# Prompt attention of a hybrid decoder step: each score matmul issued two steps ahead of its transpose instead of one, with three score buffers, and the first scores moved to an earlier place

## What is computed

```python
def masked_softmax(s, mask):
    s = jnp.where(mask, s, NEG)
    m = jnp.max(s, axis=-1, keepdims=True)
    p = jnp.where(mask, jnp.exp(s - m), 0.0)
    return p / jnp.maximum(jnp.sum(p, axis=-1, keepdims=True), 1e-30)
...
    s = jnp.einsum('bqgrd,bkgd->bqgrk', q_b, kv_b[:, :, 0], preferred_element_type=f32) * ATTN_SCALE
    s = s - slopes[None, None, :, :, None] * dist[None, :, None, None, :]
    p = masked_softmax(s, mask)
    o = jnp.einsum('bqgrk,bkgd->bqgrd', p, kv_b[:, :, 1].astype(f32))
...
    o = g[:, :, 0] * o_cmp + g[:, :, 1] * o_sel + g[:, :, 2] * o_win
```

## Time and profile before

| | us |
|---|---|
| median of 3 runs (2410.17 to 2414.91) | 2412.21 |
| the profiled execution | 2410.67 |
| its span, first to last instruction | 2409.0 |
| PE busy in the span | 2229.3 |
| the prompt attention, first to last of its jobs | 1310.0 to 1683.9 |

### The profile page before, as it was taken

How to read it: one execution, slowest core, us unless ns; L and a number is a source line. 1 busy time by engine, 2 the same in 40 slices (tenths; PEclk the granted TensorE clock), 3 DMA queues, 4 the chain that set the end, 5 groups by cost and what they waited for, 6 DMA issues and landing times. The chain is left out here.

```text
span 2409.0 us, 53122 instructions
## 1 busy us (share of the span) xinstructions
PE 2229.3 (93%) x22026; PEld 2038.8 (85%) x22026; DVE 1260.8 (52%) x2504; ACT 823.1 (34%) x1519; POOL 279.3 (12%) x430
## 2 busy tenths in 40 slices
PE   7999999999999999999998888788889769999997
PEld 6998888888888888999997666677887559999997
DVE  6345555555555553588883456565145425355454
ACT  4333334333333422222223344344223224233342
POOL 0000000000000100001004233111314410000000
PEclk9999999999999999999998899899999879999999
DMA  4322121221212222786756222211749954445564
GB/s 146 104 73 78 51 65 56 65 78 55 73 52 64 75 77 75 254 289 219 253 191 194 66 70 65 72 56 42 272 156 322 301 170 147 134 137 172 185 202 140
DMA packets 139540, 318.98 MB, mean 132 GB/s; under 512 B 28090, under 2 KB 56996, under 8 KB 138276
## 3 DMA queue, kind: packets, MB, share of 16 engines
q1 hardware_dynamic: 102148, 226.72, 29.3%
q0 software_dynamic: 17040, 55.63, 7.0%
q10 hardware_dynamic: 20112, 33.23, 4.0%
HBM read 277.77 MB, written 46.06 MB: 134 GB/s over the span
## 5 line engine op out<-in xcount | busy, mean ns | idle before, releaser
L200 PE MATMUL acc<-xh,w_hi 128*128 128x272 f32 x2944 | 657.6, 305 | 11.4 <-DVE w_lo L168 10.4
L200 PE MATMUL acc<-xh,w_lo 128*128 128x272 f32 x2944 | 616.3, 291 | 0.0
L200 PE MATMUL acc<-xl,w_hi 128*128 128x272 f32 x2944 | 616.2, 291 | 0.0
L200 PEld LDWEIGHTS acc<-xh,w_hi 128*128 128x128 f32 x2944 | 465.9, 192 | 67.2 <-issue 45.7
L200 PEld LDWEIGHTS acc<-xl,w_hi 128*128 128x128 f32 x2944 | 471.0, 192 | 0.0
L200 PEld LDWEIGHTS acc<-xh,w_lo 128*128 128x128 f32 x2944 | 468.6, 192 | 0.0
L168 DVE TENSOR_TENSOR w_lo<-w_raw,w_hi 128x1024 fp32r<-128x1024 f32 x164 | 200.2, 1223 | 206.8 <-ACT w_hi L161 200.4
L161 ACT ACTIVATE w_hi<-w_raw 128x1024 fp32r<-128x1024 f32 x188 | 198.3, 1056 | 290.2 <-PE acc L200 201.6
L2830 DVE TENSOR_TENSOR m_w_lo<-m_w,m_w_hi 128x1024 fp32r<-128x1024 f32 x96 | 117.6, 1225 | 141.0 <-ACT m_w_hi L2765 141.0
L1305 DVE SCALAR_TENSOR_TENSOR b_C<-b_rows,b_pos_s,b_C 128x512 f32<-128x512 f32 x240 | 162.4, 744 | 0.0
L2948 PE MATMUL m_acc<-m_m_hi,m_w_hi 128*128 128x272 f32 x512 | 154.0, 301 | 0.0
(11 more groups left out here) (447 smaller groups left out, 3148.7 us busy)
## 6 DMA issues: line engine op xcount, KB each, us to landing
w_raw<-in_w_all SPq DMA_DIRECT2D x168, 512.0 KB, 3.6
m_w<-in_w_mo SPq DMA_DIRECT2D x96, 512.0 KB, 4.0
b_rows<-in_cmp_rows SPq DMA_DIRECT2D x128, 256.0 KB, 3.7
w_raw<-in_w_all ACTq DMA_DIRECT2D x20, 512.0 KB, 5.3
tmp_uT<-ub ACTq DMA_DIRECT2D x35, 272.0 KB, 3.4
m_gates<-tmp_uT SPq DMA_DIRECT2D x32, 272.0 KB, 2.7
d_ring<-in_sel_k SPq DMA_DIRECT2D x64, 128.0 KB, 4.2
d_ring<-in_sel_k POOLq DMA_DIRECT2D x64, 128.0 KB, 4.3
```

Source lines behind the costliest of these rows:

```text
L200: ins = self.nc.tensor.matmul(acc[:, c, 0:HALF], w[:, k % KH, :], x[:, k, c * HALF:(c + 1) * HALF], start=(k == 0 and m == 0), stop=(k == ...
```

## The change

Scores come two steps ahead of the turn: in step v PE does `score(v+2)` and `turn(v)`, DVE `maxes(v+2)` and `scales(v+1)`, ACT `exps(v+2)`. S has three buffers in place of two (`cum` and `o` of the samples share the space of `sq` and `k2` now). The jobs C of pair 0 and the first two steps' scores are placed after 9 pieces (`SCORE_PIECES`) and the 7 further pieces between them and CT. CT of a later pair comes after the first turn of that pair in place of the last turn of the one before; `row_exps` is issued in halves over four steps; the next q and bias are loaded one step sooner. On DVE the preparation of the sample vectors is split: the norm and the sums first, the rest (`prepared`) behind `maxes(1)`. ACT takes root and sigmoids first, the two exponents after the gates. No amount of arithmetic changes.

```diff
-C_STEP, CEXP_STEP, CINV_STEP, CT_STEP = 2, 3, 5, 7
+SCORE_PIECES = 9
+C_STEP, CEXP_STEP, CINV_STEP, CT_STEP = 2, 3, 5, 0
...
-    order, gaps = [("C", 0), ("C", 1), ("S0", 0), ("S1", 0), ("CT", 0), ("CT", 1)], {}
+    order = [("C", 0), ("C", 1), ("S0", 0), ("S1", 0), ("S0", 1), ("S1", 1), ("CT", 0), ("CT", 1)]
+    gaps, first_turn = {}, len(order) - 2
...
-        if v + 1 < NV:
-            order += [("S0", v + 1), ("S1", v + 1)]
+        if v + 2 < NV:
+            order += [("S0", v + 2), ("S1", v + 2)]
...
-    n, at = {"act": 0, "dve": 0}, START_PIECES
+    n, at = {"act": 0, "dve": 0}, SCORE_PIECES
     for k, job in enumerate(order):
+        if k == first_turn:
+            at = START_PIECES
...
-        S, PT = ([sb(f"a_{n}{j}", [P, 2, SEQ]) for j in range(2)] for n in ("S", "PT"))
+        S, PT = ([sb(f"a_{n}{j}", [P, 2, SEQ]) for j in range(m)] for n, m in (("S", 3), ("PT", 2)))
...
+    def act_root(self, act):
+        f = self.nc.scalar.activation
+        act.wait_ge(self.norm_in, 1)
+        f(self.ss[:, :], self.ss[:, :], ACT.Sqrt).then_inc(self.act_done, 1)
+        f(self.gate[:, :, :], self.g, ACT.Sigmoid).then_inc(self.act_done, 1)
+
+    def act_decay(self, act):
         f = self.nc.scalar.activation
         act.wait_ge(self.cum_in, 1)
         f(self.W[:, :, :], self.cum[:, :, :], ACT.Exp, scale=DECAY_SCALE).then_inc(self.act_done, 1)
         f(self.Ei[:, :, :], self.cum[:, :, :], ACT.Exp, scale=-DECAY_SCALE).then_inc(self.act_done, 1)
-        act.wait_ge(self.norm_in, 1)
-        f(self.ss[:, :], self.ss[:, :], ACT.Sqrt).then_inc(self.act_done, 1)
-        f(self.gate[:, :, :], self.g, ACT.Sigmoid).then_inc(self.act_done, 1)
...
+        def prepared():
+            link(ts(k2[:, :, :], self.a, 1.0, None, ALU.subtract))
+            link(tt(k2[:, :, :], k2[:, :, :], self.over_t(1), ALU.mult))
+            link(stt(out=k2[:, :, :], in0=k2[:, :, :], scalar=1.0, in1=self.k, op0=ALU.add, op1=ALU.mult))
+            dve.wait_ge(self.act_done, 1)
+            link(vv.reciprocal(ss[:, :], ss[:, :]))
+            link(tt(kk[:, :, :], kraw[:, :, :], self.over_d(ss), ALU.mult))
+            vv.tensor_copy(self.Q8[:, 0, :], kk[:, 0, :])
+            link(stt(out=self.nb[:, :, :], in0=kk[:, :, :], scalar=-1.0, in1=self.a, op0=ALU.mult, op1=ALU.mult))
+            dve.sem_inc(self.ready, 1)
...
+            Z.act_root(act)
             act.wait_ge(gates_in, 16)
             f(gates[:, :, :], gates[:, :, :], ACT.Sigmoid).then_inc(gates_ready, 1)
+            Z.act_decay(act)
+            background(8)
...
+                row_exps(w, 0)
+                row_exps(w, 1)
             exps(0)
+            exps(1)
             load_rows(act, 1)
             row_turned(0)
             row_turned(1)
             for v in range(NV):
                 p, step = divmod(v, 2 * N_TILE)
-                if v + 1 < NV:
-                    exps(v + 1)
+                if v + 2 < NV:
+                    exps(v + 2)
...
-            samples_rest = Z.dve_before(dve)
+            prepared, samples_rest = Z.dve_before(dve)
             row_maxes(0)
             row_maxes(1)
             maxes(0)
+            maxes(1)
+            prepared()
             dve.wait_ge(gates_ready, 1)
             row_scales(0)
             row_scales(1)
+            scales(0)
             for v in range(NV):
+                if v + 2 < NV:
+                    maxes(v + 2)
                 if v + 1 < NV:
-                    maxes(v + 1)
-                scales(v)
+                    scales(v + 1)
...
-            background(START_PIECES)
+            background(SCORE_PIECES)
             enter(pe)
             row_scores(0)
             score(0)
+            score(1)
             row_turned(0)
             row_turned(1)
             for v in range(NV):
-                if v + 1 < NV:
-                    score(v + 1)
+                if v + 2 < NV:
+                    score(v + 2)
...
         pool.wait_ge(self.ready, 1)
-        pool.wait_ge(self.act_done, 2)
+        pool.wait_ge(self.act_done, 4)
```

More of the change, by code:

```diff
@@ L1636, in prompt_jobs @@
         gaps[len(order)] = 2 * v + 1
-        if p + 1 < N_PAIR and step in (C_STEP, CT_STEP):
-            order += [("C" if step == C_STEP else "CT", 2 * p + 2 + a) for a in range(2)]
+        if p and step == CT_STEP:
+            order += [("CT", 2 * p), ("CT", 2 * p + 1)]
+        if p + 1 < N_PAIR and step == C_STEP:
+            order += [("C", 2 * p + 2), ("C", 2 * p + 3)]
         if v in SAMPLE_JOBS:
@@ L1839, in exps, with row_exps @@
                     taken(act, (f"S{a}", v))
-                    f(S[v % 2][:, a, 0:keys(v)], S[v % 2][:, a, 0:keys(v)], ACT.Exp, scale=-1.0,
+                    f(S[v % 3][:, a, 0:keys(v)], S[v % 3][:, a, 0:keys(v)], ACT.Exp, scale=-1.0,
                       bias=mx[:, v % 4, a:a + 1], accum_out=sums[:, v % 4, a:a + 1]).then_inc(exp_done, 1)
-            def row_exps(w):
+            def row_exps(w, q):
                 background(place["C", w])
                 taken(act, ("C", w))
-                for t in range(N_TILE):
+                for t in (2 * q, 2 * q + 1):
                     f(Sc[w % 4][:, t, :], Sc[w % 4][:, t, :], ACT.Exp, scale=-1.0, bias=cmx[:, w % 4, t:t + 1],
                       accum_out=csum[:, w % 4, t:t + 1]).then_inc(c_exp, 1)
-                act.wait_ge(c_exp, N_TILE * (w + 1))
-                f(csum[:, w % 4, :], csum[:, w % 4, :], ACT.Identity, bias=tiny[:, 0:1]).then_inc(csum_ready, 1)
+                if q == 1:
+                    act.wait_ge(c_exp, N_TILE * (w + 1))
+                    f(csum[:, w % 4, :], csum[:, w % 4, :], ACT.Identity, bias=tiny[:, 0:1]).then_inc(csum_ready, 1)
             def row_turned(w):
@@ L1889, in _ @@
                 f(PT[v % 2][:, 0, 0:keys(v)], bank[:, bank_of["T0", v], 0:keys(v)], ACT.Copy).then_inc(ev_act, 1)
-                if step == 2 * N_TILE - 2 and p + 2 < N_PAIR:
+                if step == 2 * N_TILE - 3 and p + 2 < N_PAIR:
                     load_rows(act, p + 2)
-                if p + 1 < N_PAIR:
-                    if step in (CEXP_STEP, CEXP_STEP + 1):
-                        row_exps(2 * p + 2 + step - CEXP_STEP)
-                    if step == CT_STEP:
-                        row_turned(2 * p + 2)
-                        row_turned(2 * p + 3)
+                if p and step == CT_STEP:
+                    row_turned(2 * p)
+                    row_turned(2 * p + 1)
+                if p + 1 < N_PAIR and step >= CEXP_STEP and step < CEXP_STEP + 4:
+                    w, half = divmod(step - CEXP_STEP, 2)
+                    row_exps(2 * p + 2 + w, half)
                 sample_copy(v)
@@ L1913, in maxes @@
                     vec.tensor_tensor_reduce(
-                        out=S[v % 2][:, a, 0:keys(v)], in0=bank[:, bank_of[job], 0:keys(v)],
+                        out=S[v % 3][:, a, 0:keys(v)], in0=bank[:, bank_of[job], 0:keys(v)],
                         in1=bias[v // 8 % 2][:, a, SEQ - keys(v):SEQ], scale=-1.0, scalar=3e38,
@@ L1925, in scales @@
                 for a in range(2):
-                    part = S[v % 2][:, a, 0:keys(v)]
+                    part = S[v % 3][:, a, 0:keys(v)]
                     vec.tensor_scalar(part, part, coef[:, j, a:a + 1], None, ALU.mult).then_inc(scaled, 1)
@@ L1986, in _ @@
                         row_maxes(2 * p + 3)
[L1987 to L1988 removed]
+                    if step in (CINV_STEP, CINV_STEP + 2):
+                        row_scales(2 * p + 2 + (step - CINV_STEP) // 2)
                 if v >= 8 and samples_rest:
@@ L2108, in _ @@
                 turn(v)
-                if p + 1 < N_PAIR:
-                    if step == C_STEP:
-                        row_scores(p + 1)
-                    if step == CT_STEP:
-                        row_turned(2 * p + 2)
-                        row_turned(2 * p + 3)
+                if p and step == CT_STEP:
+                    row_turned(2 * p)
+                    row_turned(2 * p + 1)
+                if p + 1 < N_PAIR and step == C_STEP:
+                    row_scores(p + 1)
                 if v in SAMPLE_JOBS:
```

37 lines of the change are left out of this document (11 added, 26 removed).

## The result

The median is 2343.30 us (four runs, 2335.08 to 2344.80), against 2411.19 of the kernel before beside it: ratio 0.9709, 95% interval [0.9684, 0.9734]. It is faster by 68 us; the forecast was 2340, in a range of 2326 to 2360.

The account below looks back on a forecast made before the run. PE was taken as the bound, idling because DVE, in order, had maxes(v+1) ahead of scales(v). Start 4.4, idling 52.1 and clock 15.6 sum to 72.1 us: 2338.6 profiled, median 2340, range 2326 to 2360 for 8 in 10.

Parts of the forecast that it names:

- start: From piece 9 to the first turn: 6.7 us of waits in place of 11.2, first turn 4.4 us earlier.
- idling of the steps: PE's waits behind the first turn: 58.1 us, of which 6 stay, so 52.1 us go.
- clock: PE's half-clock stretches in the stage: 21.6 us lost, 15.6 come back; bounds 0 and 21.6.
- The chain at the start: POOL's products, third `low`, fifth rounding on ACT, first turn: PE waits 5.2 us, turns at about 1319.7.
- POOL's `low` against DVE: In the steps, 17 POOL operations that can stretch DVE's: from nothing to 34 us, taken as 4.
- for all others I leave 2.3: Clock term: 2.3 us of loss left for half-clock stretches other than the first and the one behind Y.
- if `low` hits cost more than 10: Listed sign that the forecast is wrong: hits of POOL's `low` costing more than 10 us.
- The clock behind Y: Clock term: the half-clock stretch behind job Y stays, 1.4 us of loss.
- Half gain: Rival: waits move to `values` or a bank, 28 to 40 us above the forecast, some 2374; chance 0.15.
- the waits at lines 2078 and 2057: Listed sign that the forecast is wrong: waits standing at these lines for more than 15 us.
- Slower by the clock: Rival: PE falls to 1.2 GHz at the start and stays long; half of the work so gives 2446; chance 0.03.
- All of it: Variant without residue: 4.4 + 58.1 + 21.6 = 84 us, 2328; within the forecast's 0.80 with its start and residue variants.

Follow-up runs that it names:

- The two controls: The changed kernel again, unaltered, in the second and third series: 2339.46 us (ratio 0.9710) and 2340.79 us (ratio 0.9711).
- the experiment with one moved line: The kernel before with only DVE's scales(v) put ahead of maxes(v+1), scores still one step ahead: 2361.18 us, ratio 0.9797.
- The run with short later `low`: The changed kernel with POOL's lows of this stage from the fourth on cut to 8 of 1024 columns: 2328.36 us, ratio 0.9665.
- the control: The changed kernel unaltered, beside the run with short later `low` in the third series: 2340.79 us, ratio 0.9711.
- the same swap: DVE's scales put ahead of maxes: in the kernel before 2361.18 us (ratio 0.9797), in the changed kernel 2349.39 us (ratio 0.9752).
- the first control: The changed kernel unaltered, in the second series: 2339.46 us (2334.76 to 2344.84), ratio 0.9710.

## Why the prediction was right

By its own terms, the profiled execution of after against that of before:

| term | forecast | measured | from |
|---|---|---|---|
| start | 4.4 | 3.85 | 1324.15 - 1299.50 = 24.65 less 20.80 |
| idling of the steps | 52.1 | 48.5 | 58.86 less 292.94 - 282.60 = 10.34 |
| clock | 15.6 | 18.3 | 300.89 less 282.60 |
| sum | 72.1 | 70.7 | 384.40 less 313.74 |

The two controls give 4.3 and 4.0 for the start, 46.9 and 47.4 for the idling, 18.0 and 17.8 for the clock. So the sum of the forecast is nearer than its terms: over the three traces it has 3.6 to 5.2 us too much for the idling and 2.2 to 2.7 too little for the clock, and these cancel in part, which is luck.

**What bounds it.** Right: DVE's order held the turns, and the experiment with one moved line showed it by itself. The chain at the start came as forecast, link by link.

**The steps.** Of the waits behind the first turn the forecast left 6 us: 2 at `values` in tile 2, from DVE's new order, and 4 from `low`. The run with short later `low` keeps the two apart. There 1.7 us stay at `values` in four waits, three of them of 0.4 in tile 2, so the first size was right. What goes with the `low`, against the control, is 5.1 us at `values` and 2.0 us at C for a bank that DVE's copy of O frees, a place that I had not listed.

**The mis-sized step** is "POOL's `low` against DVE", taken as 4. Leaving out the later ones gave 12.4 us of the median and 11.2 in the traces: 7.2 of idle time, nearly twice what I took, and 3.9 of clock, which I had put into another term, with "for all others I leave 2.3". By my own list ("if `low` hits cost more than 10") this step was wrong. The sum hardly moved, because less stayed at half clock than I had left: 18.3 us came back for the 15.6 of the forecast.

**The clock behind Y.** I kept 1.4 us of loss there. The spell was 10.2 us before (1381 to 1391), 13.6 in the first trace of the changed kernel (1360 to 1373) and 10.2 in both controls. Without it PE is busy for 3.6 to 3.8 us less behind the first turn, but the stretch is only some 1 us shorter. That loss at half clock comes back in full was assumed for every stretch; here most of it does not.

**The rivals.** Half gain is out: the waits at lines 2078 and 2057 are 5.6 and 2.2 us. Slower by the clock is out: 0.97 from 1325 to 1610 (forecast over 0.96), last O at 1610 (forecast near 1612). All of it, 2328, is what the kernel comes near only without the hits (2325 and 2328).

**What stays open.** The forecast took the median of the changed kernel 1.5 us above the profiled time; its three medians (2343.3, 2339.5, 2340.8) lie 4 to 8 above the first profiled execution. The traces show spells of half clock behind waits of about 1 us in some executions and not in others. In the eleven traces with C after piece 9 the clock fell behind the waits at C and at the second scores in eight and stayed in three, and the waits at C do not tell them apart (0.78 to 1.22 us in the eight, 0.75 to 1.02 in the three). Why the clock falls behind one and not behind the next was not settled.

## What to carry to other kernels

Where an engine in order serves two consumers, list for each of its blocks who waits and how much work that one has left; the block with less goes first. This can turn with the depth of the pipeline: the same swap won 48 us at one step of lead and lost 10 at two. A hit of 2 us by another engine's operation is priced with the half clock that follows the wait it makes (here 7.2 us idle and 3.9 of clock), and a clock loss is priced by the wait right behind it: if another engine sets the pace there, PE at full clock mostly waits. And before busy and idle time of two traces are compared, the stretches that the edit leaves alone are taken out: a spell of half clock at the start turned 2.9 us of waiting into busy time.

## What was not expected of the hardware

A DVE operation on two numbers per partition took 0.2 us alone and 2.20 beside POOL's 2.37. Behind a wait of 2.45 us PE ran at 1.2 GHz (granted clock 0.50) for 3.4 us. In eight of eleven traces it did so behind a wait of about 1 us (0.94 and 1.22 in the two controls) and one of 0.82 that began 1.4 us after the first had ended, in three it did not. Some 11 us of dense 8-column matmuls, with PE busy all the time, also led to 1.2 GHz: the clock fell 2.8 us into them in the first trace and 3.8 in the first control, and rose again 13.6 and 10.2 us later; with three pieces of 272 columns among them it stayed at 2.4.
